# Seven half-size products for four more projection blocks, decay levels by halves under copied masks, and a later start of the rotation on GpSimd

## What is computed

```
p = (h @ w_in).astype(jnp.float32)
hq, hf, hi, hgate, rq, rk, rv, rgate = jnp.split(p, splits, axis=-1)
f = lb + (1.0 - lb) * jax.nn.sigmoid(hf)
...
        diff = bcum[:, :, :, None, :] - bcum[:, :, None, :, :]
        decay = jnp.exp(jnp.where(mask[:, :, None], diff, -jnp.inf))
        scores = jnp.einsum('bhtd,bhsd,bhtsd->bhts', qc, kc, decay)
        out = jnp.einsum('bhts,bhsv->bhtv', scores, vc) \
...
    rq = rope(rq, RET_HEADS)
    rk = rope(rk, RET_HEADS) * RET_DK ** -0.5
```

## Time and profile before

| | |
|---|---|
| median of 3 runs | 1440.77 us (1439.57 to 1441.41) |
| the profiled execution: its own time | 1433.36 us |
| its span, first to last instruction | 1431.6 us |
| granted TensorE clock, mean of the span | 0.943 |
| granted clock from 68 to 173 us | 1.00 |
| PE busy | 1234.8 us, 86% of the span |
| DVE, ACT, POOL busy | 645.2, 243.0, 83.4 us |

### The profile page before, as it was taken

One profiled execution on the slowest core, in us unless ns is written; L12 is line 12 of the kernel. 1 busy time (PEld: TensorE's weight loads), 2 busy tenths in 40 slices (PEclk: granted clock), 3 DMA queues, 4 the chain that ended last, 5 costly groups with the idle time before them and its releaser, 6 DMA issues.

```text
span 1431.6 us, 15460 instructions
## 1 busy us (share of the span) xinstructions
PE 1234.8 (86%) x6555; PEld 787.3 (55%) x6555; DVE 645.2 (45%) x832; ACT 243.0 (17%) x483; POOL 83.4 (6%) x81
## 2 busy tenths in 40 slices
PE   8999999999999999999999999999664664646647
PEld 5855848995446775997445878555231221312212
DVE  6478426567865752666886674315110100101001
ACT  2421212330011331222002142013000000000000
POOL 0046201000000001000001200000000000000000
PEclk9999999999999999999999999999986877877778
DMA  9533334448963324446993533397999999999997
GB/s 359 181 121 118 118 130 165 177 177 299 350 230 118 118 102 162 143 158 231 352 353 118 176 134 145 134 404 298 425 428 428 427 429 427 429 427 428 428 424 263
DMA packets 94391, 376.96 MB, mean 263 GB/s; under 512 B 7248, under 2 KB 7920, under 8 KB 82416
## 3 DMA queue, kind: packets, MB, share of 16 engines
q1 hardware_dynamic: 93728, 373.84, 67.2%
q0 software_dynamic: 576, 2.10, 0.4%
q10 hardware_dynamic: 16, 0.00, 0.0%
HBM read 374.88 MB, written 1.05 MB: 263 GB/s over the span
## 4 chain that ended last, share of the span: by engine, by line
PE 70%; DMA 21%; DVE 4%; ACT 2%; issue 1%; POOL 0%; DVEq 0%; SPq 0%; POOLq 0%; ACTq 0%
PE PS L998 13%; PE PS L951 12%; PE PS L733 12%; PE PS L776 8%; DMA weights<-in_w 8%; PE PS L716 7%; DMA arena<-in_w 6%; PE PS L1215 6%; DMA proj_rows<-in_w 4%; PE PS L1253 3%; DMA normalised<-in_w 2%; PE PS L986 2%; PE PS L677 2%; PE PS L919 1%; PE PS L859 1%
## 5 line engine op out<-in xcount | busy, mean ns | idle before, releaser
L1215 PE MATMUL PS<-weights,x_rows 128*32 128x512 f32 x368 | 132.2, 725 | 45.2 <-DMA proj_rows<-in_w 23.5
L998 PE MATMUL PS<-weights,arena 128*128 128x512 f32 x384 | 167.4, 592 | 0.0
L733 PE MATMUL PS<-weights,normalised 128*128 128x256 f32 x720 | 160.5, 380 | 3.3 <-DVE weights L1791 2.6
L733 PEld LDWEIGHTS PS<-weights,normalised 128*128 128x128 f32 x720 | 135.7, 190 | 25.4 <-issue 6.1
L2366 DVE TENSOR_TENSOR x_rows<-x_rows,PS 128x512 f32<-128x512 f32 x8 | 8.4, 1048 | 289.0 <-PE PS L1215 289.0
L1215 PE MATMUL PS<-arena,x_rows 128*32 128x512 f32 x256 | 95.8, 711 | 42.0 <-DMA weights<-in_w 28.3
L776 PE MATMUL PS<-weights,arena 128*128 128x512 f32 x288 | 125.4, 594 | 2.7 <-ACT arena L1430 1.4
L998 PEld LDWEIGHTS PS<-weights,arena 128*128 128x128 f32 x384 | 72.8, 190 | 90.9 <-issue 90.9
L1215 PE MATMUL PS<-proj_rows,x_rows 128*32 128x512 f32 x240 | 79.5, 710 | 43.5 <-DMA normalised<-in_w 22.8
L716 PE MATMUL PS<-weights,normalised 128*128 128x512 f32 x256 | 112.2, 594 | 3.1 <-ACT normalised L1415 1.7
L951 PE MATMUL PS<-normalised,weights 128*128 128x128 f32 x896 | 106.9, 275 | 0.0
(11 more groups left out here) (350 smaller groups left out, 1740.0 us busy)
## 6 DMA issues: line engine op xcount, KB each, us to landing
weights<-in_mlp_w SPq DMA_DIRECT2D x32, 2048.0 KB, 8.5
weights<-in_w SPq DMA_DIRECT2D x32, 2048.0 KB, 34.2
arena<-in_w SPq DMA_DIRECT2D x24, 2048.0 KB, 36.1
proj_rows<-in_w SPq DMA_DIRECT2D x16, 2048.0 KB, 34.9
weights<-in_ev_w_in SPq DMA_DIRECT2D x10, 2048.0 KB, 9.3
weights<-in_w_in SPq DMA_DIRECT2D x10, 2048.0 KB, 7.9
proj_rows<-in_w_ada SPq DMA_DIRECT2D x16, 1024.0 KB, 11.0
early_weights<-in_w SPq DMA_DIRECT2D x8, 2048.0 KB, 36.1
```

The costliest lines, as they stand in the source:

```text
L733: last = mm(at, lhs[:, k, :], rhs[:, k, :], start=(first and k == 0), stop=(k == 3), skip_group_check=not first)
L998: last = mm(PS[:, bank, :], lhs[:, k0 + i, rows], rhs[:, i, :], start=(g == 0 and i == 0), stop=(g == NGRP - 1 and i == 1))
L1215: last = mm(PS[CAP * x:CAP * (x + 1), 4 + kind, :], XG[:, k, CAP * x:CAP * (x + 1)], w[:, k, :], start=(k == 0), stop=(k == KT - 1), tile_ ...
```

## The change

Four things change, all in the first mixer. Blocks 4 to 7 are done as `seven_block`, with their sums on DVE and partial reads on ACT. For levels 1 to 8 only the halves that the level uses are scaled: the left halves of k and the right halves of q, 512 elements each, both by DVE (`level_rows`); POOL does none of it, and at the program's start it fills the buffers of scaled rows with zeros. `masked` becomes one `copy_predicated` from PS into the scores under the mask. POOL's rotation waits for the last level's rows (`hg_qs` 8).

```
+            nc.gpsimd.memset(AR[:, 6 * K1:9 * K1], 0.0).then_inc(sem("half_ready"), 1)
...
             pool.wait_ge(sem("proj_taken"), 6)
+            pool.wait_ge(sem("hg_qs"), 8)
...
             for b, levels in ((4, (1, 2)), (5, (3, 4)), (6, (5, 6)), (7, (7, 8))):
-                proj_block(B_EV_IN + b)
+                seven_block(B_EV_IN + b)
...
+            for b, levels in ((4, (1, 2, 3, 4)), (5, (5, 6)), (6, (7, 8)), (7, ())):
+                at = B_EV_IN + b
+                if b > 4:
+                    part(at, 0)
+                    part(at, 1)
+                    finish(at - 1, (b - 1) * NB, *kinds[b - 1])
+                    part(at, 2)
+                    for n in levels:
+                        level_exp(n)
+                    part(at, 3)
+                else:
+                    level_exp(1)
+                    part(at, 0)
+                    part(at, 1)
+                    level_exp(2)
+                    part(at, 2)
+                    level_exp(3)
+                    part(at, 3)
+                    level_exp(4)
...
             part_sums(B_EV_IN + 3, 3 * NB)
+            col_sums(B_EV_IN + 4)
+            last_sum(B_EV_IN + 4)
...
-                    link(v.tensor_tensor(t, src, mask, ALU.mult))
-                    tell(v.tensor_tensor(SC, SC, t, ALU.add), "hg_masked", n + 1)
+                    mask = midb(MX[:, M_LEV + n * P:M_LEV + (n + 1) * P].bitcast(mybir.dt.uint32), 8)
+                    tell(v.copy_predicated(SC, mask, src), "hg_masked", n + 1)
+
+            def level_rows(n):
...
+                link(v.tensor_tensor(level_half(KS[i], n, 0), level_half(KTT, n, 0), level_half(ex, n, 0), ALU.mult))
+                tell(v.tensor_tensor(level_half(QS[i], n, 1), level_half(QT, n, 1), level_half(ex, n, 1), ALU.mult),
+                     "hg_qs", n)
...
+            dve.wait_ge(sem("half_ready"), 2)
+            level_rows(1)
+            diffs(3)
+            level_rows(2)
+            diffs(4)
+            next_sums(5)
+            part_sums(B_EV_IN + 4, 4 * NB)
+            for b in (5, 6, 7):
+                n = 2 * b - 9
+                masked(n)
+                masked(n + 1)
+                level_rows(n + 2)
+                if n + 4 <= 8:
+                    diffs(n + 4)
+                level_rows(n + 3)
+                if n + 5 <= 8:
+                    diffs(n + 5)
+                next_sums(b + 1)
+                part_sums(B_EV_IN + b, b * NB)
+            masked(7)
```

More of the change, by code:

```diff
@@ L85 @@
 UPS = [[base + g for g in range(1, FF // NB)] for base in MLP_BASES]
-SEVEN = ([B_EV_IN + b for b in (1, 2, 3, 8, 9)] + UPS[0] + [B_OD_IN + b for b in (1, 2, 3, 5)]
+SEVEN = ([B_EV_IN + b for b in range(1, EV_IN)] + UPS[0] + [B_OD_IN + b for b in (1, 2, 3, 5)]
          + UPS[1] + B_IN2_AT[1:])
@@ L249, in block_program, with level_half @@
         TMP = ar(10 * K1, K1)
+        def level_half(v, n, side):
+            if n == 8:
+                return v[:, :, side * P:(side + 1) * P]
+            m = 1 << (n - 1)
+            return v.rearrange("p h (n x m) -> p (h n) x m", x=2, m=m)[:, :, side, :]
         ROWS = ar(9 * K1, 2 * P)
@@ L846, in level @@
                     pe.wait_ge(sem("hg_qs"), n)
-                    pe.wait_ge(sem("hg_ks"), n)
                     q, k = QS[(n - 1) % 2], KS[(n - 1) % 2]
@@ L1383, in level_exp @@
                 a(EX[(n - 1) % 2], EX[(n - 1) % 2], ACT.Exp).then_inc(sem("hg_exp"), 1)
[L1385 to L1391, removed]
+            for b, levels in ((4, (1, 2, 3, 4)), (5, (5, 6)), (6, (7, 8)), (7, ())):
[17 more added lines that the diff above has]
+                    level_exp(4)
+            part(B_EV_IN + 8, 0)
+            part(B_EV_IN + 8, 1)
+            finish(B_EV_IN + 7, 7 * NB, *kinds[7])
             act.wait_ge(sem("hg_prod"), 9)
             a(S01, PS[:, 4, :].rearrange("p (h t) -> p h t", h=4), ACT.Copy).then_inc(sem("hg_s01"), 1)
-            parts(B_EV_IN + 8)
+            part(B_EV_IN + 8, 2)
+            part(B_EV_IN + 8, 3)
             finish(B_EV_IN + 8, 8 * NB, ACT.Silu)
@@ L1881, in diffs @@
                 ex = EX[(n - 1) % 2]
-                if n >= 3:
-                    dve.wait_ge(sem("hg_ks"), n - 2)
                 if n <= 7:
@@ L1912, in masked, with next_sums @@
                 src = PS[:, bank:bank + 2, :].rearrange("p b (h t) -> p (b h) t", h=4)
-                mask = midb(MX[:, M_LEV + n * P:M_LEV + (n + 1) * P], 8)
                 if n == 0:
+                    mask = midb(MX[:, M_LEV:M_LEV + P], 8)
                     tell(v.tensor_tensor(SC, src, mask, ALU.mult), "hg_masked", 1)
                 else:
-                    t = TMP.rearrange("p (g t) -> p g t", g=8)
-                    link(v.tensor_tensor(t, src, mask, ALU.mult))
-                    tell(v.tensor_tensor(SC, SC, t, ALU.add), "hg_masked", n + 1)
+                    mask = midb(MX[:, M_LEV + n * P:M_LEV + (n + 1) * P].bitcast(mybir.dt.uint32), 8)
+                    tell(v.copy_predicated(SC, mask, src), "hg_masked", n + 1)
+            def level_rows(n):
+                i = (n - 1) % 2
+                ex = EX[i].rearrange("p (a b) -> p a b", a=4)
+                dve.wait_ge(sem("hg_exp"), n)
+                if n >= 3:
+                    dve.wait_ge(sem("hg_prod"), n - 1)
+                link(v.tensor_tensor(level_half(KS[i], n, 0), level_half(KTT, n, 0), level_half(ex, n, 0), ALU.mult))
+                tell(v.tensor_tensor(level_half(QS[i], n, 1), level_half(QT, n, 1), level_half(ex, n, 1), ALU.mult),
+                     "hg_qs", n)
+            def next_sums(b):
+                col_sums(B_EV_IN + b)
+                last_sum(B_EV_IN + b)
             diffs(1)
```

## The result

| | before | changed |
|---|---|---|
| median (range) | 1439.55 us (1433.16 to 1442.25), 22 runs | 1431.22 us (1425.78 to 1437.57), 22 runs |
| ratio, 95% interval | | 0.9948 [0.9937, 0.9959] |
| profiled execution, span | 1431.6 us | 1427.6 us |
| POOL busy | 83.4 us | 60.7 us |

Faster, by 0.52%; the forecast was 0.49% (1433.8 from 1440.8). The median of 1431.22 lies at the lower edge of the range on record (1431.2 to 1438.8), in part because the kernel before has a median of 1439.55 in 22 runs and had 1440.77 in three. The spans of the two profiled executions differ by 4.0 us only, and why that is less is part of what the runs looked at.

What follows compares the result with a forecast made beforehand. PE was taken to bound the kernel up to the 26th slice, loads after it. 6.6 - 1.4 + 1.3 + 0.5 = 7.0 us less, from a median of 1440.8 to 1433.8, range 1431.2 to 1438.8.

Steps and rivals of the forecast that it cites:

- Four blocks, 6.6 us: PE, blocks 4 to 7: each goes from 13.73 to 12.09 us as a seven-product block, 6.6 us less.
- New wait of 1.4 us inside block 4: PE in block 4 waits 1.4 us for ACT's first part read, queued behind table load and first exponential.
- DVE keeps up: DVE's round of 14.5 us stays 1.2 below PE's 15.66; before the rounds DVE is just in time.
- dear-copy rival: Copy costs about the pair's 2.45, or halves 1.22; DVE sets the pace, block 9 at 153.6 to 155.6, 1438.8; chance 0.14.
- The copy at 1.22: DVE's copy under a mask takes 1.22 us, like the multiply of PS by the mask; no row showed it.
- The slower rival: DVE's copy takes over 2.7 us, turning at 2.6 to 2.9; block 9 at 159 to 161.5, 1444.5; chance 0.07.
- The halves at 0.69: DVE's half-row scalings of 512 elements take 0.69 us at every level, like the exponents; upper bound 1.22.
- Block 8's sums early, 1.31 us: DVE's weight sums for block 8 end well ahead, so PE's wait of 1.31 us before it goes.
- Rotation from 120.9 to 143.5: POOL's rotation ends before PE's first transposes at 146.3; new wait costs 0, at most 0.5 us.
- Last wait, 0.5 us less: PE's wait ahead of the second transposes falls from 1.68 to 1.2 us, as ACT's squares start earlier.
- The fill, 2.3 us at no cost: POOL's zero fill, from 8.45 at the start, takes 2.3 us, at most 6.8, and costs PE 0.
- The gain reaches the end: A first-mixer gain near 100 us reaches the end whole; rival of no gain at the end, 1440.8, chance 0.07.

Runs made afterwards that it cites:

- The three undone parts: Three kernels, each the changed kernel with one part undone: POOL's wait before the rotation, the copy under a mask, the half rows; 1.0009, 0.9993, 1.0020 against before.
- the mask experiment: Changed kernel with the copy under a mask as multiply and add again (two instructions); 0.9993 against before, 5.5 us more from cumulative sums to second transposes.
- the second fill: From the changed kernel with POOL's zero fill done twice, one after the other, near 8.4 us; DVE's scaling ended at 11.62, nothing behind moved.
- the second timing: Changed kernel run once more, unchanged, on another chip than the kernels with parts undone; 0.9970 [0.9954, 0.9986] against before, median 1434.21 us.
- padded variants: Kernel before with four or eight unused 128 x 512 products on PE ahead of block 9, 3.4 or 6.9 us later; with eight, experts start at 1000.7.
- the one with the early rotation: Changed kernel without POOL's wait for the last level's rows, so the rotation starts earlier; 1.0009 [0.9993, 1.0025] against before, median 1440.37 us.

## Why the prediction was right, step by step

- *Four blocks, 6.6 us.* A block is 12.09 us in the chain; 6.56 as forecast. Taken back alone, it costs 4.99, since what block 4 loses goes with it: it takes 13.50 us (68.52 to 82.02), 1.41 over a block without a wait, and starts 0.18 late, 1.59 together.
- *New wait of 1.4 us inside block 4.* As a cost to PE it is the forecast's 1.4 (13.50 for 12.09); the idle time itself is 1.07. That the cost came out to a tenth is luck, since the 0.3 beyond the idle time lie in the starts of the matmuls around the wait, which I had not counted. For the idle time I took the exponential and the read one behind the other in full, and they overlap by 0.1; PE also began the block 0.18 late. The 0.18 is a term that I had as zero ("just in time").
- *DVE keeps up.* Right, and narrowly. The round I had at 14.5 us is 14.6 in the trace (from the copies at 85.51 to those at 100.13) against 15.66. The three undone parts each make DVE late, and each costs 5.5 to 7.2 us of S. The dear-copy rival had the mechanism and the size: 153.6 to 155.6 for block 9, where the pair gave S + 5.5, that is about 155.4 on the scale of the changed trace. The rotation slipped by 6.4 us and not by the 3 that the rival has, and PE waited for it.
- *The copy at 1.22.* Mis-sized by 0.12: 1.34. It hid, seven of them, in DVE's slack. The slower rival's 2.6 us was far.
- *The halves at 0.69.* Right for every stride.
- *Block 8's sums early, 1.31 us.* Right: no wait there.
- *Rotation from 120.9 to 143.5.* From 121.56 to 144.73; PE reached it at 146.44. No cost, as taken. The margin was 1.7 us; in the mask experiment, where the rotation starts 6.4 us later, PE waits 1.87 for it.
- *Last wait, 0.5 us less.* 0.40.
- *The fill, 2.3 us at no cost.* 2.66, no cost. The rule of the Trainium skill that I weighed (SBUF — State Buffer, Who interferes with whom) agrees with the traces as I read it: the scaling of the second tile took 1.30 us and ended at 11.65, 0.55 behind the fill, and the sum beside the second fill was not slowed.
- *The gain reaches the end.* Yes: the time is 0.9948 for the changed kernel and 1.0012 when 6.87 us are put back, and the last part takes 437.8 to 439.2 us in every trace, whenever it starts. In the first pair of traces only half of it is visible, because of the clock's fall, which I had not in the sum. The interval of the second timing, [0.9954, 0.9986], is 2.0 to 6.6 us and just misses 6.9; that of the first, 5.9 to 9.1, takes it in. The sum of 7.0 us is borne out by S (6.94); that the first timing gave 0.52% for the 0.49% of the forecast is closer than the timing can tell, since the second gave 0.30%.

What stays open: how often the clock falls at the column modulations in the timed executions, and whether the changed kernel brings it more often. All ten traces of the changed kernel and its variants have at least one fall, of the four of the kernel before and its padded variants one. If 11 falls were dealt out blindly to 14 traces, such a split would come up once in some 90 times, so chance alone is a poor account of it, and no run here shows another. If the changed kernel had one fall more than before in every timed execution, the gain would be 6.9 - 3.3 = 3.6 us, which the second timing allows and the first excludes. Two things on record speak against so large an effect. Most timed executions of the kernel before lose time as well: its two traces without a fall took 1433.4 and 1433.0 us, its medians are 1439.55 and 1438.16. And the fastest of 22 executions each, 1433.16 and 1425.78, lie 7.4 us apart; the fastest of the changed kernel is 3.6 us below its profiled execution, which had one fall.

## What to carry to other kernels

When a cheaper product needs sums on another engine, the engine's round must be counted against the product's round to a tenth of a microsecond: here 14.6 against 15.7, and each of three small reliefs of DVE was a condition: without any one of them the cheaper products brought nothing over a kernel that has the reliefs alone. A second engine's independent work should start when the first engine's short instructions are over, since a turn lost costs the same for 256 elements as for 1024. And a part read that frees PE is better placed ahead of an exponential, above all of one that waits for someone else; three such moves on ACT made S 1.8 us shorter, which the timed runs can't tell from nothing.

## What the runs showed that I had not expected

- A wait of PE costs more than its length. Behind waits of 3.57 and 3.56 us eight half-size matmuls took 2.79 and 3.37 us instead of 1.97, and the granted clock of the 8.4 us behind the first was 0.80, so part of it at 1.2 GHz. Behind waits of 1.07 and 1.63 us they took 1.99 or less. The wait of 1.87 us in the mask experiment also had a fall of the clock behind it, 0.62 from 155 to 163 us. Even without a fall, at clock 1.00, a wait costs some tenths more than its length: 1.41 us for the 1.07 in block 4, and 1.47 for the 1.31 ahead of block 8 in the kernel before.
- At a stretch of 32 matmuls of a single column the clock fell in some executions, at one layer's or the other's or both. At the second layer's it cost 3.3 us each time (eight traces), at the first layer's 2.7 to 2.9 in four traces and 4.7 in the one with the early rotation. The Trainium skill (TensorE: Matmul & The Clock Gate, Part 1) says that the monitor behind the clock runs freely and does not start with the kernel. By that rule such a fall comes by chance at a fixed place of the program; the traces agree as far as one kernel had it once here and once there, but ten of ten against one of four is more than this rule alone accounts for.
- Five DVE instructions of 256 elements, 0.29 to 0.43 us alone, took 1.25 to 1.45 beside steps of the rotation, and a copy of one operand was among them, not only those with two.
